# Samples' attention in a hybrid decoder step: rows of eight tokens in the gathers, and the products with the values between the turning of the third and the fourth group

## The reference, cut to what matters

```python
ckv_past = cache_ckv[layer, page_table].reshape(Bs, past_len, KV_LORA)     # 8 x 8192 x 256
kr_past = cache_krope[layer, page_table].reshape(Bs, past_len, QK_ROPE)    # 8 x 8192 x 32
sp = (einsum('bqhr,bkr->bhqk', ql, ckv_past) + einsum('bqhd,bkd->bhqk', qr, kr_past)) * scale
p = softmax(concatenate([sp, s], axis=-1), axis=-1)
o = einsum('bhqk,bkr->bqhr', p[..., :n_past], ckv_past) + ...
```

## Time and profile before

| | us |
|---|---|
| median of three runs | 2445.48 |
| the profiled execution's own time | 2449.44 |
| its span | 2447.6 |
| PE busy, share of the span | 2265.7 (93%) |
| DVE busy | 1013.3 (41%) |
| ACT busy | 810.7 (33%) |
| POOL busy | 410.8 (17%) |
| first and last start of the turning of rotary keys (L1434) | 837.8, 1143.7 |

### The profile page before, as it was taken

The page is one execution under the profiler, slowest core; times in us unless marked ns, Lnnn a source line. Parts: engine busy times, 40 slices in busy tenths (PEclk is TensorE's granted clock), DMA queues, the critical chain, the costliest instruction groups (busy, mean ns, idle before and its releaser), DMA issues.

```text
span 2447.6 us, 38563 instructions
## 1 busy us (share of the span) xinstructions
PE 2265.7 (93%) x16195; PEld 2008.0 (82%) x16195; DVE 1013.3 (41%) x1797; ACT 810.7 (33%) x1392; POOL 410.8 (17%) x464
## 2 busy tenths in 40 slices
PE   4999989999998999888999798979999999899993
PEld 4999989997544676665899676859999999899993
DVE  3452133334376654444451846471111111255556
ACT  5221222222344444444243334441111111144542
POOL 0000011101200277774043510200000000000000
PEclk9999989999999999999899999999999999999997
DMA  4122233332200277775431242121111111101121
GB/s 132 44 87 87 87 108 113 111 92 99 85 1 1 111 233 233 235 235 155 147 130 35 69 158 83 35 79 51 43 45 49 43 51 43 56 26 45 47 93 69
DMA packets 186495, 223.38 MB, mean 91 GB/s; under 512 B 17977, under 2 KB 149510, under 8 KB 185622
## 3 DMA queue, kind: packets, MB, share of 16 engines
q1 hardware_dynamic: 155254, 114.33, 15.2%
q0 software_dynamic: 31136, 107.56, 13.7%
HBM read 191.88 MB, written 29.98 MB: 91 GB/s over the span
## 4 chain that ended last, share of the span: by engine, by line
PE 74%; DVE 9%; POOL 6%; ACT 5%; issue 4%; DMA 1%; POOLq 0%; ACTq 0%; SPq 0%; DVEq 0%
PE ps L1535 26%; PE ps L1097 18%; PE ps L1828 10%; PE ps L1585 2%; POOL mem_high L990 2%; POOL mem_low L990 2%; POOL mem_high L991 1%; POOL mem_low L991 1%; PE ps L1445 1%; PE ps L1261 1%; PE ps L1734 1%; PE ps L1374 1%; PE ps L1379 1%; PE ps L1475 1%; ACT mem_low L2045 1%
## 5 line engine op out<-in xcount | busy, mean ns | idle before, releaser
L1097 PE MATMUL ps<-stream_first,early_first 128*128 128x344 f32 x912 | 298.7, 328 | 4.3 <-DVE H_short L2472 3.0
L1097 PE MATMUL ps<-H_short,early_first 128*128 128x344 f32 x912 | 294.2, 323 | 0.0
L1097 PE MATMUL ps<-stream_first,ring_short 128*128 128x344 f32 x912 | 293.8, 322 | 0.0
L1535 PE MATMUL ps<-stream_first,sel_short 128*128 128x344 f32 x1152 | 252.1, 323 | 8.0 <-DVE H_short L2861 3.6
L1535 PE MATMUL ps<-H_short,sel_short 128*128 128x344 f32 x1152 | 251.2, 322 | 1.6 <-DVE ring_short L2867 1.6
L1535 PE MATMUL ps<-stream_first,ring_short 128*128 128x344 f32 x1056 | 228.8, 320 | 0.0
L1535 PEld LDWEIGHTS ps<-stream_first,sel_short 128*128 128x128 f32 x1152 | 195.3, 188 | 13.2 <-DVE H_short L2861 5.8
L1535 PEld LDWEIGHTS ps<-H_short,sel_short 128*128 128x128 f32 x1152 | 196.9, 190 | 2.1 <-DVE ring_short L2867 2.0
L2867 DVE TENSOR_TENSOR ring_short<-ring_raw,sel_short 128x1024 fp32r<-128x1024 f32 (+1 forms) x64 | 70.0, 1093 | 296.3 <-ACT sel_short L2116 296.3
L1097 PEld LDWEIGHTS ps<-stream_first,early_first 128*128 128x128 f32 x912 | 174.3, 191 | 13.1 <-ACT mem_high L1953 6.1
L1535 PEld LDWEIGHTS ps<-stream_first,ring_short 128*128 128x128 f32 x1056 | 177.5, 188 | 0.0
(11 more groups left out here) (532 smaller groups left out, 4283.9 us busy)
## 6 DMA issues: line engine op xcount, KB each, us to landing
ring_raw<-w_ffn_in SPq DMA_DIRECT2D x44, 512.0 KB, 3.7
ring_raw<-w_in SPq DMA_DIRECT2D x37, 512.0 KB, 3.8
ring_raw<-w_ffn_out SPq DMA_DIRECT2D x16, 704.0 KB, 4.7
branch_gates<-mem_high POOLq DMA_DIRECT2D x16, 516.0 KB, 4.6
chunks_apart<-mem_high POOLq DMA_DIRECT2D x12, 516.0 KB, 2.9
mem_high<-chunks_apart POOLq DMA_DIRECT2D x8, 768.0 KB, 5.8
mem_low<-branch_gates SPq DMA_DIRECT2D x2, 2064.0 KB
mem_high<-branch_gates SPq DMA_DIRECT2D x1, 4128.0 KB
```

Source lines behind the costliest of these rows:

```text
L1097: mm = pe.matmul(ps[:, bank, 0:TN], w[:, k], x[:, k, j * TN:(j + 1) * TN], start=(k == 0 and q == 0), stop=(k == KT - 1 and q == 2))
L1535: mm = pe.matmul(ps[:, s + j, 0:TN], w[:, k], x[k][:, j * TN:(j + 1) * TN], start=(k == 0 and q == 0), stop=(k == kts - 1 and q == 2))
```

## The change

It has two parts.

**Gathers.** A row is eight tokens: a gather of latents brings 128 rows of 8 KB into two groups at once, a gather of rotary keys 128 rows of 1 KB. There are four indirect DMAs per unit, 128 in all. The row numbers are worked out in another way (two instructions for each 32 partitions in place of one, and a wait between them), there are half as many of them, and the semaphore's values follow.

**Order on PE.** In each step but the last, `turn(v, 3)` is issued after `values(u)` instead of ahead of it. The orders of ACT and DVE are untouched.

```diff
             def gather(u, s, more=True):
                 if more:
-                    n = (u + 1) * GROUPS
+                    n = (u + 1) * 2
                     pool.wait_ge(idxu_ok, u + 1)
-                    pool.tensor_copy(idxu[(s + 1) % 4], idx[:, bass.ds(n, GROUPS)]).then_inc(idxu_ok, 1)
-                for g in range(GROUPS):
-                    at = bass.IndirectOffsetOnAxis(ap=idxu[s][:, g:g + 1], axis=0)
-                    pool.indirect_dma_start(ukv[s][:, g].rearrange("p r c -> p (r c)"), None, ckv_rows, at).then_inc(kv_in[s], 16)
-                    pool.indirect_dma_start(ukr[s][:, g], None, kr_rows, at).then_inc(kv_in[s], 16)
+                    pool.tensor_copy(idxu[(s + 1) % 4][:, 0:2], idx[:, bass.ds(n, 2)]).then_inc(idxu_ok, 1)
+                for h in range(2):
+                    at = bass.IndirectOffsetOnAxis(ap=idxu[s][:, h:h + 1], axis=0)
+                    pool.indirect_dma_start(ukv[s][:, 2 * h:2 * h + 2].rearrange("p g r c -> p (g r c)"), None, ckv_rows, at).then_inc(kv_in[s], 16)
+                    pool.indirect_dma_start(ukr[s][:, 2 * h:2 * h + 2].rearrange("p g x -> p (g x)"), None, kr_rows, at).then_inc(kv_in[s], 16)
...
                 turn_probs(u)
                 if not last:
                     turn(v, t, 2)
-                    turn(v, t, 3)
                 values(u, s)
                 if not last:
+                    turn(v, t, 3)
                     scores(v, vb)
...
                     for q in range(4):
                         rows = slice(32 * q, 32 * q + 32)
-                        ins = dve.tensor_scalar(idx[rows], tbl[rows].rearrange("p (n q) -> p n q", q=4)[:, :, q], float(PAGE // 4),
-                                                rowno[rows], ALU.mult, ALU.add)
+                        pages = tbl[rows].rearrange("p (n q) -> p n q", q=8)
+                        step.mark(dve.tensor_scalar(idx_first[rows], pages[:, :, 2 * q], rowno[rows, 1:2], rowno[rows, 0:1], ALU.mult, ALU.add))
+                        step.join()
+                        ins = dve.scalar_tensor_tensor(out=idx[rows], in0=pages[:, :, 2 * q + 1], scalar=rowno[rows, 2:3],
+                                                       in1=idx_first[rows], op0=ALU.mult, op1=ALU.add)
```

More of the change, by code:

```diff
@@ L195, in build @@
         QR = small(4 * NB * AH).rearrange("p (r b h) -> p r b h", r=4, b=NB)
-        idx = small(NB * NPG // 4).bitcast(U32)
+        idx = small(NB * NPG // 8).bitcast(U32)
+        idx_first = small(NB * NPG // 8)
         idxu = [small(4).bitcast(U32) for _ in range(4)]
-        rowno = small(1)
+        rowno = small(3)
         mx = small(4).rearrange("p (n j) -> p n j", j=2)
@@ L977, in _ @@
             pool.dma_start(out["krope_sample"][0].rearrange("b t r -> (b t) r"), cks[:, KL:]).then_inc(latents_out, 16)
-            ckv_rows = d["cache_ckv"][0].rearrange("n (a r) c -> (n a) (r c)", r=4)
-            kr_rows = d["cache_krope"][0].rearrange("n (a r) c -> (n a) (r c)", r=4)
+            ckv_rows = d["cache_ckv"][0].rearrange("n (a r) c -> (n a) (r c)", r=8)
+            kr_rows = d["cache_krope"][0].rearrange("n (a r) c -> (n a) (r c)", r=8)
             def gather(u, s, more=True):
                 if more:
-                    n = (u + 1) * GROUPS
+                    n = (u + 1) * 2
                     pool.wait_ge(idxu_ok, u + 1)
-                    pool.tensor_copy(idxu[(s + 1) % 4], idx[:, bass.ds(n, GROUPS)]).then_inc(idxu_ok, 1)
-                for g in range(GROUPS):
-                    at = bass.IndirectOffsetOnAxis(ap=idxu[s][:, g:g + 1], axis=0)
-                    pool.indirect_dma_start(ukv[s][:, g].rearrange("p r c -> p (r c)"), None, ckv_rows, at).then_inc(kv_in[s], 16)
-                    pool.indirect_dma_start(ukr[s][:, g], None, kr_rows, at).then_inc(kv_in[s], 16)
+                    pool.tensor_copy(idxu[(s + 1) % 4][:, 0:2], idx[:, bass.ds(n, 2)]).then_inc(idxu_ok, 1)
[3 more added lines that the diff above has]
+                    pool.indirect_dma_start(ukr[s][:, 2 * h:2 * h + 2].rearrange("p g x -> p (g x)"), None, kr_rows, at).then_inc(kv_in[s], 16)
             pool.wait_ge(latents_out, 16 * 7)
@@ L998, in _ @@
             pool.wait_ge(pe_event, EV["sample_h_turned"])
-            pool.tensor_copy(idxu[0], idx[:, 0:GROUPS]).then_inc(idxu_ok, 1)
+            pool.tensor_copy(idxu[0][:, 0:2], idx[:, 0:2]).then_inc(idxu_ok, 1)
             for s in range(UPS):
@@ L1003, in _ @@
                 if s == 3:
-                    pool.wait_ge(kv_in[0], 128)
+                    pool.wait_ge(kv_in[0], 64)
                 gather(s, s)
@@ L1008, in _ @@
                     pool.wait_ge(dec_values_done, b * UPS + (s - UPS + 1))
-                    pool.wait_ge(kv_in[(s + 1) % 4], b * 128 + (0 if s < 3 else 128))
+                    pool.wait_ge(kv_in[(s + 1) % 4], b * 64 + (0 if s < 3 else 64))
                     gather(b * UPS + s, s)
@@ L1012, in _ @@
                 pool.wait_ge(dec_values_done, (NB - 2) * UPS + s + 1)
-                pool.wait_ge(kv_in[(s + 1) % 4], (NB - 1) * 128 + (0 if s < 3 else 128))
+                pool.wait_ge(kv_in[(s + 1) % 4], (NB - 1) * 64 + (0 if s < 3 else 64))
                 pool.wait_ge(idxu_ok, (NB - 1) * UPS + s + 1)
@@ L1431, in turn_rope @@
             def turn_rope(v, s):
-                pe.wait_ge(kv_in[s], (v - s) * 32 + 128)
+                pe.wait_ge(kv_in[s], (v - s) * 16 + 64)
                 for g in range(GROUPS):
@@ L3225, in shape_constants @@
         "c_rope": np.concatenate([table, table], 0).reshape(rope, -1),
-        "c_row": (i % 32).astype(np.float32)[:, None],
+        "c_row": np.stack([i % 16, (i % 32 < 16) * 16, (i % 32 >= 16) * 16], 1).astype(np.float32),
     }
```

## The result

The changed kernel took 2482.44 us (median of four runs, 2479.13 to 2483.63), beside 2444.76 us for the kernel before in the same comparison. The ratio is 1.0147, with an interval from 1.0126 to 1.0168: 37.7 us slower. The forecast was 2467.6 with a range up to 2474, so the sign was right and the size was not. The profiled executions differ by 34.2 us (span 2481.8 against 2447.6); the traces can explain these 34.2, and the other 3.5 us of the medians' difference lie in how the runs scatter (the kernel before: 2442.74 to 2446.78 in this comparison, 2449.44 for its profiled execution).

A forecast was written before the change was run, and what follows sets the result against it. PE's own 9.58 us step was taken as the bound until 928 us, then POOL's 10.07 us per unit. Swap 31 x 0.99 = 30.7 us less 8.6 gave +22.1, from 2445.48 to 2467.6 us, range 2452 to 2474.

The forecast's parts named there:

- The order on PE: Term for PE's step: scores wait openly for group 3's copy; 4.64 us against 3.65, so 0.99 us more per step.
- The bound from above: Upper limit on the swap's price per PE step: 1.3 us, if the probabilities' copy came another 0.3 late.
- signs of being wrong: PE steps below 9.9 us, L1457 (the scores) waiting less than 0.5 us, or L1434 (rotary turning) still waiting for landings.
- I leave the clock at 2.4 GHz: PE's clock in the new step: stays at 2.4 GHz with 9.19 of 10.57 us busy, 87%.
- POOL's pace: From 928 us PE runs at POOL's gather cycle, 10.07 us per unit; ending this limit gains 8.6 us.
- four gathers at the old price each: POOL's issue: four gathers of 1.25 us plus a copy of about 0.36, 5.4 us per unit.
- transfers that keep up: Gather queues: a 9.58 us step wants 246 GB/s; 368 GB/s was seen from 838 to 856 us, so transfers hide.
- the row numbers at no cost: DVE's row-number operations: four more of at most 0.33 us, with waits some 2 us, in idle time, costing nothing.
- the copy hides: Rival ahead of PE's scores: group 3's copy finds cover, leaving only the gathers' gain, 2436.9 us; chance 0.07.
- half the price: Rival in PE's step: the swap costs 0.5 us per step, +6.9 us in sum, 2452.4 us; chance 0.08.
- the bound by transfers: Rival in the gathers: 8 KB rows move under 223 GB/s; at 200 GB/s about +57 us, 2502; chance 0.03.
- rival 4: PE's clock falls within the steps: about +270 us for the whole stage, 2717, or 8 us per step; chance 0.02.

The follow-up runs named there:

- constants: The changed kernel with PE's loop over the samples written out, so that every wait of PE is for a constant: 2476.57 us.
- gathers_only: The changed kernel with the old order on PE, group 3 turned ahead of the values, keeping the 8 KB rows: 2441.57 us, ratio 0.9974.
- rope_late_short_rows: The kernel before, eight gathers kept, with ACT's copy of the rotary keys moved behind the turned probabilities: 2445.61 us, ratio 1.0005.

## Why the prediction was wrong

**The step that failed is the size of one term of the sum, the 0.99 us per step in "The order on PE".** The runs show 1.42 (11.01 - 9.59, and 10.52 - 9.10). Term by term, from the changed kernel's step:
- the start of group 2's turning to the values: 861.07 - 860.05 = 1.02, forecast 0.97;
- the values' hold on PE: 862.93 - 861.07 = 1.86, forecast 1.75. The 1.75 was the distance to scores; behind the values stands a turning now, and why it starts 0.11 us later no run tests;
- the turning of group 3 to its last result: 1.09, as forecast;
- the wait for its copy: 1.07, forecast 0.83. This is the largest miss. The 0.83 was read from unit 0, whose waits are for constants; in the loop the sequencer works out three more waits' values in the open. Outside the loop the 0.83 is there to the hundredth, and in constants it is there in every step.

These give 0.05 + 0.11 + 0.24 = 0.40 of the missing 0.43 us. Times 28 steps the miss is 12 us. The bound from above, 1.3 us, left the 0.83 as it was and allowed only for a late copy of the probabilities, and the range used only 1.2 of it. The signs of being wrong that the prediction named all point to a smaller price (steps below 9.9 us, a wait below 0.5 us, waits for landings). None of them came, and none could have caught a price that was larger.

**The second miss is in the last two steps.** The forecast gave them the same 0.99 and a clock of 2.4 GHz throughout. They took 14.3 us each where the kernel before had 11.56, 2.7 each. Turning and values ran partly at the lower clock. "I leave the clock at 2.4 GHz" failed there and held elsewhere in the stage: the granted clock is 1.00 from 838 to 1165 us. Only a part of the 2.7 is the swap's. Beside gathers_only, whose clock falls in both steps too, the swap costs 14.36 - 13.17 = 1.19 and 14.23 - 13.19 = 1.04 us there; the other 1.6 us of each step come with the lower clock, which the long rows alone also have. The forecast took these two steps from one row, and did not see that in the kernel before the first of the two was filled by a wait for a landing.

**The sum with measured terms:** 28 x 1.42 = 39.8, the first step outside the loop 10.39 - 9.20 = 1.2, the last two 2.8 + 2.7 = 5.5, together 46.5 us. Against this stands the end of POOL's pace. The forecast took PE's own step as 9.58 everywhere and found 8.6 us. Every fourth is 9.20, so PE's own pace over the stage is 8 x 9.20 + 21 x 9.58 + 2 x 11.56 = 297.9 us, and the difference to 309.2 is 11.3. 46.5 - 11.3 = 35.2, measured in the stage 35.3. So the forecast's 8.6 was too small by 2.7 us, and this miss took a part of the other back: of the swap's 46.5 us it had 30.7.

**What was right:** POOL's pace as the bound of the kernel before after 928 us (rope_late_short_rows shows it again, with a faster PE); four gathers at the old price each; transfers that keep up; the row numbers at no cost (eight operations of 0.33 us each, in an idle time of DVE); the swap as a new wait ahead of the scores, on the path and larger than the gain; the sign. One reading behind the transfers was wrong, though nothing came of it: of the 368 GB/s from 838 to 856 us the gathers' own queue moved 3.96 MB, 220 GB/s, and another queue 2.64 MB, so that window did not show 246 GB/s for gathers. gathers_only does: 19.17 MB on the gathers' queue from 856 to 928 us, 266 GB/s, and no wait for a landing. Of the rivals, that the copy hides is refuted by the 28 waits, half the price by the 1.42, and the bound by transfers by gathers_only. The fall of the clock took place in two steps, not in the rest; rival 4's 8 us for such a step was 1.6.

## What to carry to other kernels

A wait that has always been hidden costs more when it is laid open than the copy that it waits for: here 1.07 us for a copy of 0.69. In a loop add the working out of every further wait's value, here 0.08 us each, and read the price from a place inside the same loop. Work that fills the time of a copy is worth its place: moving the turning of one group out from under its cover cost 1.42 us in each of 28 steps. A faster feeder and a shorter step of its consumer pay together: the long rows alone gave 6 us and the shorter chain on ACT alone gave nothing, but the two together gave 23. And name signs of being wrong on both sides of a forecast.

## What the runs showed of the hardware

- An indirect DMA of 128 rows took POOL 0.96 us with rows of 8 KB and 0.95 with rows of 1 KB, the same as with 4 KB and 512 B. So with 128 rows the price did not depend on the bytes in a row; no run has another number of rows.
- PE's sequencer spent 0.24 us on three waits in a row against values from a loop's register, behind a first one that it had to wait for, so some 0.08 us each; with constants the same place took 0.83 us and not 1.07, with one such wait 0.88.
- From the last transpose of a group to the first matmul that reads its copy PE was idle for 0.83 us; DVE's copy of 128x512 took 0.69 us of it, ACT's 0.60.
- PE's granted clock fell inside the last two steps of the changed kernel (0.89 and 0.83 in the mean of their windows), which have pauses of 2.4 and 0.83 us. It held at 1.00, which is 2.4 GHz, through 28 steps with pauses of up to 0.39 and 1.07 us, and in the kernel before also through a pause of 2.4 us.
